# Two layers of a streaming encoder on one core: the MLP's down projection in passes of 512 hidden columns, with seven block products in place of eight

## What is computed

```python
D_MODEL, D_FF = 1024, 4096          # 1024 + 8 * 16 = 1152 tokens = 9 tiles of 128
def sq_relu_mlp(x, w_up, w_down):
    return jnp.square(jax.nn.relu(x @ w_up)) @ w_down
...
hp = hp + sq_relu_mlp(rmsnorm(hp, norm_ffn[i]), ffn_w_up[i], ffn_w_down[i])
hs = hs + sq_relu_mlp(rmsnorm(hs, norm_ffn[i]), ffn_w_up[i], ffn_w_down[i])
```

## Time and profile before

| | us |
|---|---|
| median of 3 runs | 2989.47 |
| lowest and highest run | 2988.71, 2990.20 |
| span of the profiled execution | 2987.3 |
| PE busy | 2903.7 (97%) |
| PEld busy | 2644.4 (89%) |
| DVE busy | 1504.3 (50%) |
| ACT busy | 996.1 (33%) |
| POOL busy | 683.6 (23%) |

### The profile page before, as it was taken

One profiled execution on the slowest core, in us unless ns is written; L12 is line 12 of the kernel. 1 busy time (PEld: TensorE's weight loads), 2 busy tenths in 40 slices (PEclk: granted clock), 3 DMA queues, 4 the chain that ended last, 5 costly groups with the idle time before them and its releaser, 6 DMA issues. The chain is left out here.

```text
span 2987.3 us, 44886 instructions
## 1 busy us (share of the span) xinstructions
PE 2903.7 (97%) x17447; PEld 2644.4 (89%) x17447; DVE 1504.3 (50%) x2576; ACT 996.1 (33%) x1796; POOL 683.6 (23%) x482
## 2 busy tenths in 40 slices
PE   8999999989999999999999999989999999999998
PEld 8889877679998999999989899978999999999997
DVE  4489799842544444434452266536253434343435
ACT  3377678761321212121231144433132121212122
POOL 2221110112212121111122244445221111111111
PEclk9999999999999999999999999999999999999999
DMA  4422612342211111111104333266211111111111
GB/s 146 110 69 72 170 36 43 64 151 75 66 42 42 42 42 42 42 42 42 42 14 149 104 98 107 89 237 217 73 64 42 42 42 42 42 42 42 42 42 64
DMA packets 196024, 222.38 MB, mean 74 GB/s; under 512 B 27745, under 2 KB 172065, under 8 KB 195890
## 3 DMA queue, kind: packets, MB, share of 16 engines
q1 hardware_dynamic: 155346, 156.08, 17.1%
q10 hardware_dynamic: 40544, 64.49, 6.6%
HBM read 170.58 MB, written 49.95 MB: 74 GB/s over the span
## 5 line engine op out<-in xcount | busy, mean ns | idle before, releaser
L918 DVE TENSOR_TENSOR h<-mlp_dn_acc,h 128x512 f32<-128x512 f32 x576 | 397.4, 691 | 339.6 <-PE mlp_dn_acc L873 339.6
L907 DVE TENSOR_TENSOR mlp_sq<-mlp_relu 128x384 f32<-128x384 f32 x192 | 163.6, 852 | 541.6 <-ACT mlp_relu L794 541.6
L858 PE MATMUL acc<-mid_xT_hi,mid_w_hi 128*128 128x384 f32 x752 | 251.4, 334 | 0.6 <-PEq L572 0.6
L858 PE MATMUL acc<-mid_xT_hi,mid_w_lo 128*128 128x384 f32 x752 | 251.4, 334 | 0.0
L858 PE MATMUL acc<-mid_xT_lo,mid_w_hi 128*128 128x384 f32 x752 | 251.3, 334 | 0.0
L873 PE MATMUL mlp_dn_acc<-mid_w_hi,mlp_hid_hi 128*128 128x512 f32 x576 | 224.6, 390 | 0.0
L873 PE MATMUL mlp_dn_acc<-mid_w_lo,mlp_hid_hi 128*128 128x512 f32 x576 | 224.5, 390 | 0.0
L873 PE MATMUL mlp_dn_acc<-mid_w_hi,mlp_hid_lo 128*128 128x512 f32 x576 | 224.4, 390 | 0.0
L873 PE MATMUL mlp_dn_acc<-end_w_lo,mlp_hid_hi 128*128 128x512 f32 x576 | 224.4, 390 | 0.0
L873 PE MATMUL mlp_dn_acc<-end_w_hi,mlp_hid_lo 128*128 128x512 f32 x576 | 224.3, 389 | 0.0
L873 PE MATMUL mlp_dn_acc<-end_w_hi,mlp_hid_hi 128*128 128x512 f32 x576 | 224.1, 389 | 0.0
(11 more groups left out here) (402 smaller groups left out, 7373.2 us busy)
## 6 DMA issues: line engine op xcount, KB each, us to landing
spare_w<-in_ffn_w_up ACTq DMA_DIRECT2D x30, 1024.0 KB, 5.3
mid_w_raw<-in_ffn_w_down ACTq DMA_DIRECT2D x15, 1024.0 KB, 5.0
end_w_raw<-in_ffn_w_down ACTq DMA_DIRECT2D x15, 1024.0 KB, 5.0
proj_w_raw<-in_a_w_in SPq DMA_DIRECT2D x8, 1024.0 KB, 6.0
mid_w_raw<-in_b_w_in SPq DMA_DIRECT2D x6, 1024.0 KB, 6.1
spare_w<-in_b_w_in SPq DMA_DIRECT2D x5, 1024.0 KB, 6.0
hd<-h SPq DMA_DIRECT2D x9, 512.0 KB, 9.5
state_g<-gg SPq DMA_DIRECT2D x9, 512.0 KB, 8.0
```

The source lines that it names most:

```text
L858: mm = pe.matmul(up_acc[:, u % 3, 0:GW], w_up_s[a][:, k, j * P:(j + 1) * P], x_s[c][:, k, g * GW:(g + 1) * GW], start=(n == 0), stop=(n == ...
L907: dve.tensor_tensor(sq[:, u % 2, :], relu[:, u % 2, :], relu[:, u % 2, :], ALU.mult)\
L918: dve.tensor_tensor(cols, dn_acc[:, v % 3, :], cols, ALU.add).then_inc(added, 1)
```

## The change

In 7 of 8 passes per phase, the down projection of the 1024 prompt tokens is made by a scheme with seven block products. A pass now takes 512 hidden columns (`FC` = 4 blocks of 128), and there are `NCH` = 8 passes; the loop covers six of them.

- The pass's down weights are cut in four blocks of 256 hidden by 512 output columns (B11, B12, B21, B22), the hidden block of 512 by 1024 tokens in four blocks A11 to A22 of 256 hidden by 512 tokens. Seven products of blocks or of sums of blocks (`H_OF`, `W_OF`) give what eight plain ones give. One product is four units (`t`) of 6 matmuls of 512 columns; products 1, 4 and 6 go on in the banks of the product before without clearing them. What is shared between outputs is collected in `U` over the passes and added to `h` in the last pass (12 adds of 128x512). The tile of sample tokens is made plainly: one unit more in products 0, 1, 5 and 6, in the `up_acc` banks.
- DVE makes four sums of weight blocks (`w_sum`) and four of hidden blocks (`h_sum`), 128x1024 each, both operands in SBUF; the low halves of the weights of products 0 and 1 (`weight_low`) and of all seven hidden operands (`hidden_low`), also 128x1024 with both operands in SBUF; four `sample_low` of 128x128; and 31 adds of 128x512.
- POOL makes the low halves of the weights of products 2 to 6 (128x1024 each) and of four blocks of up weights (128x8x128 each).
- ACT squares in place in float32 (`evacuate`), and makes the high halves of what is multiplied: two 128x1024 copies per product, four copies for the up weights, four of 128x128 for the sample tile.
- `up_acc` has two banks in place of three, `dn_acc` four.
- All loads of the phase are issued by SP, in the order `dn(0)` (two of 1 MB), `up(1)` (1 MB), the norm's gamma, and then pass by pass. ACT waits for both loads of `dn` before it evacuates unit 1.
- The last pass stays plain: 36 units of 6 matmuls, with the hidden operands and the weights in halves.
- Outside the phase only the places of buffers change (`early_1` and `gg_last` are freed earlier; `s_hi` of `mlp1` lies in `early_0`).

The core of the diff (indentation shortened):

```diff
-    NCH = FF // CW
-    FB = CW // P
-    UU = NG * FB
-    DU = NT * (D // 512)
+def mlp_phase(nc, name, sh, h, w_up, w_down, next_gamma, next_w=None, y=None, banks=None, pre=0, s_hi=None):
+    FC, W2, TB = 4, D // 2, NT_P // 2
+    NCH = FF // (FC * P)
+    UORD = ((0, 0), (1, 0), (0, 1), (0, 2), (1, 1), (1, 2), (2, 0), (2, 1), (2, 2), (3, 0), (3, 1), (3, 2))
+    UU = len(UORD)
+    AFTER = {f: max(u for u, (ff, _) in enumerate(UORD) if ff == f) + 1 for f in range(FC)}
+    NP = 7
+    ADDS = (5, 5, 4, 4, 4, 4, 5)
+    DU = sum(ADDS)
+    done_by = [sum(ADDS[:k]) for k in range(NP + 1)]
+    S_END = DU * (NCH - 1)
+    FIRST_HALF = [(0, t) for t in (0, 1, 2, 3, 4, 5, 6, 7, 8)] + [(1, t) for t in (8, 0, 1, 2, 3, 4, 5, 6, 7)]
+    N1 = len(FIRST_HALF)
...
+        up_acc = TwoSlots(*banks[:2])
+        dn_acc = TwoSlots(*(z if z is not None else b.ps(f"dn_acc{i}", [P, 512]) for i, z in enumerate(banks[2:])))
...
+        B11, B12, B21, B22 = raw_a[:, :, 0:W2], raw_a[:, :, W2:D], raw_b[:, :, 0:W2], raw_b[:, :, W2:D]
+        A11, A12, A21, A22 = hid[:, 0:2, 0:W2], hid[:, 2:4, 0:W2], hid[:, 0:2, W2:SEQ], hid[:, 2:4, W2:SEQ]
+        W_OF = (B11, B21, B11, B12, B21, t1[:, :, :], B22)
+        H_OF = (A11, A12, A11, s3, A22, A21, A12)
...
+    def up(s):
+        sp.dma_start(up_raw, up_src(s)).then_inc(up_in, 16)
+    def dn(i):
+        sp.dma_start(raw_a, dn_src(i, 0)).then_inc(dn_in, 16)
+        sp.dma_start(raw_b[:, :, :], dn_src(i, 1)).then_inc(dn_in, 16)
+    def body(i, first, last):
+        if not first:
+            sp.wait_ge(up_lo_done, FC * i)
+            up(2 * i + 1)
+        if not last or next_w is not None:
+            sp.wait_ge(up_lo_done, FC * i + 2)
+            if last:
+                sp.dma_start(up_raw, next_w.rearrange("(k p) n -> p k n", p=P)).then_inc(up_in, 16)
+            else:
+                up(2 * i + 2)
+        if not last:
+            sp.wait_ge(w_lo26_done, (NP - 2) * i + NP - 2)
+            dn(i + 1)
+    dn(0)
+    up(1)
     tail.load_gamma(sp)
+    passes(sp, body)
...
+    def evacuate(i, u, first):
+        f, g = UORD[u]
+        if not (first and u < pre):
+            act.wait_ge(up_done, UU * i + (u + 1 - pre))
+        if g < 2:
+            pieces_of = ((hid[:, f, g * GW:(g + 1) * GW], 0, GW),)
+        else:
+            if not (first and f < 2):
+                act.wait_ge(s_lo_done, FC * i + (f - 1))
+            pieces_of = ((hid[:, f, 2 * GW:SEQ], 0, 2 * P), (s_raw[:, f % 2, :], 2 * P, GW))
+        for dst, c0, c1 in pieces_of:
+            last = act.activation(dst, up_acc[:, u % 2, c0:c1], ACT.Relu)
+        last.then_inc(up_out, 1)
+        act.wait_ge(up_out, UU * i + (u + 1))
+        for dst, c0, c1 in pieces_of:
+            last = act.activation(dst, dst, ACT.Square)
+        last.then_inc(squared, 1)
...
+        evacuate(i, 0, first)
+        act.wait_ge(dn_in, 32 * i + 32)
+        if not first:
+            act.wait_ge(dn_done, DU * i)
+        weights(w_hi[:, 0, :, :], B21 if last else B11)
+        evacuate(i, 1, first)
+        weights(w_hi[:, 1, :, :], B22 if last else B21)
+        evacuate(i, 2, first)
+        evacuate(i, 3, first)
+        up_weights(i, 2)
+        sample(i, 0)
+        evacuate(i, 4, first)
+        act.wait_ge(squared, UU * i + 5)
+        hidden(0, A11)
+        evacuate(i, 5, first)
+        up_weights(i, 3)
+        sample(i, 1)
+        if last:
+            hidden(1, A21)
+        for u in (6, 7, 8):
+            evacuate(i, u, first)
+        if last:
+            weights(quarters(up_hi, 0), B11.rearrange("p f (q c) -> p f q c", c=P))
+        else:
+            up_weights(i, 4)
+        sample(i, 2)
+        evacuate(i, 9, first)
+        evacuate(i, 10, first)
+        if not last:
+            act.wait_ge(squared, UU * i + 11)
+            hidden(1, A12)
+        evacuate(i, 11, first)
+        if last:
+            weights(quarters(up_hi, 1), B12.rearrange("p f (q c) -> p f q c", c=P))
+        sample(i, 3)
+        if last:
             return
+        up_weights(i, 5)
+        for k in range(2, NP):
+            act.wait_ge(dn_done, DU * i + done_by[k - 1])
+            if k in (2, 6):
+                act.wait_ge(s_done, 4 * i + (3 if k == 2 else 4))
+            hidden(k % 2, H_OF[k])
+            if k in (2, 4):
+                act.wait_ge(w_sum_done, 4 * i + (3 if k == 2 else 4))
+            weights(w_hi[:, k % 2, :, :], W_OF[k])
...
+    def up_weights(i, f):
+        pool.wait_ge(up_hi_done, FC * i + (f - 1))
+        pool.tensor_tensor(up_half(up_lo, f % 2), up_half(up_raw, f % 2), up_half(up_hi, f % 2).bitcast(F32), ALU.subtract)\
+            .then_inc(up_lo_done, 1)
     def body(i, first, last):
+        up_weights(i, 2)
+        up_weights(i, 3)
         if not last or next_w is not None:
+            up_weights(i, 4)
+            up_weights(i, 5)
+        if not last:
+            for k in range(2, NP):
+                pool.wait_ge(w_hi_done, NP * i + k + 1)
+                pool.tensor_tensor(w_lo[:, k % 2, :, :], W_OF[k], w_hi[:, k % 2, :, :].bitcast(F32), ALU.subtract)\
+                    .then_inc(w_lo26_done, 1)
...
+            if not (first and u < 2):
+                pe.wait_ge(up_out, UU * i + (u - 1))
...
+    def product(dst, lhs, rhs, onto=False):
+        n = 0
+        for f in range(2):
+            for a, c in TERMS:
+                mm = pe.matmul(dst, lhs(c, f), rhs(a, f), start=(n == 0 and not onto), stop=(n == 2 * len(TERMS) - 1),
+                               skip_group_check=onto)
+                n += 1
+        return mm
...
+        for k in range(NP):
+            if k < 2:
+                pe.wait_ge(w_lo01_done, 2 * i + k + 1)
+            else:
+                pe.wait_ge(w_lo26_done, (NP - 2) * i + k - 1)
+            pe.wait_ge(h_lo_done, NP * i + k + 1)
+            if k == 5:
+                pe.wait_ge(up_out, UU * i + UU)
+                sample(k, 1, 0)
+            for t in range(TB):
+                if k >= 1:
+                    pe.wait_ge(added, DU * i + done_by[k - 1] + t + 1)
+                elif not first:
+                    pe.wait_ge(added, DU * i - ADDS[NP - 1] + t + 1)
+                product(dn_acc[:, t, :], lambda c, f: h_s[c][:, k % 2, f, t * P:(t + 1) * P],
+                        lambda a, f: w_s[a][:, k % 2, f, :], k in (1, 4, 6)).then_inc(dn_done, 1)
+            if k == 0:
+                pe.wait_ge(s_lo_done, FC * i + 2)
+                pe.wait_ge(up_out, UU * i + UU - 1)
+                sample(k, 0, 0).then_inc(dn_done, 1)
+            if k == 1:
+                pe.wait_ge(s_lo_done, FC * i + FC)
+                pe.wait_ge(added, DU * i + done_by[1])
+                sample(k, 0, 1, True).then_inc(dn_done, 1)
+            if k == 6:
+                sample(k, 1, 1, True).then_inc(dn_done, 1)
...
+    def adds(i, k, first):
+        n = DU * i + (done_by[k] + 1)
+        for t in range(TB):
+            dst = (U[:, t, :], cols(t, 0), U[:, t, :], cols(TB + t, 1), cols(TB + t, 0), cols(TB + t, 1), cols(t, 1))[k]
+            add(n + t, dst, dn_acc[:, t, :], first and k == 0)
+        if k in (0, 1, 6):
+            add(n + TB, cols(NT_P, (1, 0, 0, 0, 0, 0, 1)[k]), up_acc[:, k // 6, :])
...
+        dve.wait_ge(dn_in, 32 * i + 32)
+        w_sum(t1[:, :, :], B12, B11)
+        dve.wait_ge(w_sum_done, 4 * i + 1)
+        w_sum(B12, B22, B12)
+        weight_low(NP * i + 1, w_lo[:, 0, :, :], B11, w_hi[:, 0, :, :])
+        dve.wait_ge(w_lo01_done, 2 * i + 1)
+        w_sum(B11, B22, t1[:, :, :])
+        weight_low(NP * i + 2, w_lo[:, 1, :, :], B21, w_hi[:, 1, :, :])
+        dve.wait_ge(w_sum_done, 4 * i + 3)
+        dve.wait_ge(w_lo01_done, 2 * i + 2)
+        w_sum(B21, B21, B11)
+        sample_low(i, 0)
+        dve.wait_ge(squared, UU * i + 6)
+        h_sum(s3, A11, A21)
+        hidden_low(NP * i + 1, 0, A11)
+        sample_low(i, 1)
+        sample_low(i, 2)
+        dve.wait_ge(squared, UU * i + UU)
+        dve.wait_ge(s_done, 4 * i + 1)
+        h_sum(A21, A21, A22, ALU.add)
+        hidden_low(NP * i + 2, 1, A12)
+        dve.wait_ge(s_done, 4 * i + 2)
+        dve.wait_ge(h_lo_done, NP * i + 1)
+        h_sum(A11, A21, A11)
+        sample_low(i, 3)
+        dve.wait_ge(s_done, 4 * i + 3)
+        dve.wait_ge(h_lo_done, NP * i + 2)
+        h_sum(A12, A12, A11)
+        adds(i, 0, first)
+        for k in range(2, NP):
+            hidden_low(NP * i + k + 1, k % 2, H_OF[k])
+            adds(i, k - 1, first)
+        adds(i, NP - 1, first)```

How the instructions stand. First PE: one turn of the loop held 144 matmuls of 384 columns and 108 of 512, twice per 512 hidden columns; now it holds 288 and 192. DVE, in the loop of `mlp0`, from the end of the up part to the first operand of the down part's product 2 (`mlp_hid` is the hidden block, `mlp_both_u` is `U`, `mlp_h_lo` the low halves; L1110 is `h_sum`, L1104 `hidden_low`, L1096 `sample_low`, L1117 an add). Before:

```order
L906 REGISTER_ALU
```

(47 more changed lines are left out.)

246 lines of the change are left out of this document (130 added, 116 removed).

## The result

The changed kernel takes 2974.7 us (median of four runs, 2970.2 to 2978.4) against 2989.1 for the kernel before (2988.1 to 2990.2): 14.4 us less, ratio 0.9952 (95% interval 0.9936 to 0.9964). It is faster, as forecast, but by 14 us where the forecast had 32. The profiled execution is the slowest of the four, 2978.4 us with a span of 2976.6. It goes with the 2987.3 us of the earlier trace rows, so the two profiles are 10.7 us apart.

What follows compares the result with a forecast made beforehand. PE, busy 97% of the span, was taken to bound the kernel. Span 2987.3 - 76.3 (matmuls) + 33.6 (waits before product 1) + 10.5 (entries) = 2955.1 us, median 2957; 8-in-10 range 2919 to 2984.

Steps and rivals of the forecast that it cites:

- the side that had 0.86: Whole kernel: the measured time would be faster than before, chance 0.86, against 0.04 for same and 0.10 for slower.
- the forecast's own range: Whole kernel: 2945 to 2973 us, from a product 1 wait of 1.8 to 3.3 and entries of 8 to 15; chance 0.57.
- The matmuls: Down part: 24 matmuls fewer per pass at 0.227 us each, 5.45 us per pass, 76.3 us saved over 14 passes.
- The wait between products 0 and 1: Before product 1, PE waits 2.4 us per pass for DVE's first add, delayed by POOL's up block; 33.6 us in all.
- The alternation: Before product 1, queued POOL and DVE instructions take turns, so POOL's 2.40 us up block gets in between DVE's.
- The products after it: Products 2 to 6: operands are ready before PE comes, nothing lost, with 0.7 us in hand.
- case 3: Products 2 to 6: DVE falls behind POOL, 3.6 us more waiting per pass, 3007 us, slower than before; chance 0.10.
- The entries: Start of each phase: PE waits for ACT 0.96 us, then 4.3 us; 10.5 us over both phases, between 8 and 15.
- The clock: PE's granted clock in the passes and at the entries: the sum had no term for a drop behind waits.
- The case that did: Behind the 2.4 us wait in every pass, PE's clock drops, 1.6 us lost each: +22, 2979 us; chance 0.06.

## Why the prediction was wrong in its size

The result lies within the range (2919 to 2984) and on the side that had 0.86, but outside the forecast's own range (2945 to 2973).

**The matmuls.** Right in their number, 336 fewer, and a little too high in their worth: 72.4 us with the waits and drops taken away, for 76.3. A price of 0.227 us for every matmul left out that a group at the start of a product costs more (43.9 us of down matmuls per pass for the 43.6 forecast).

**The wait between products 0 and 1.** Right in its place, cause and number. 14 times 2.18 to 2.23 us, 30.7 us for 33.6. The 0.2 us less for each is of the order of what DVE saves on instructions in a row (1.14 us from one to the next, where one lasts 1.23). The alternation was read from the earlier trace rows, at other sizes and in another phase, and it held. The Trainium skill's rule (SBUF — State Buffer, "Who interferes with whom") agrees with the 3.42 us row, and with the 1.22 that is left when GpSimd is moved.

**The products after it.** Right: no wait. The reason that case 3 stays away is stronger than the one given. With the wait gone too, DVE met POOL in half of the passes and took its lead back each time.

**The entries.** Right in their length: 10.8 us for 10.5.

**The clock: this is the step that failed.** The sum charged nothing for it. The case that did was one of all or nothing, every pass or none, with a chance of 0.06. It came in part: 8 of 14 waits were followed by a drop (12.8 us), and both entries by a longer one, together 5.2 us. That is 18 us that the sum had at nothing, and most of what the forecast missed.

The two phases can be closed on the profiled executions. Each stretch below goes from PE's third up unit (the time it was ready for it) to the last down matmul; the first two are the kernel before, the others the changed one:

```profile
774.30:1568.70 794.40, 791.00 (x4033) 720.10 (x4032) 348.04 (x496) 172.28 (x252) 154.63 (x49) 1.00 0.13 43
2189.80:2979.10 789.30, 788.72 (x3985) 720.42 (x3984) 342.04 (x487) 164.40 (x239) 149.51 (x48) 1.00 0.14 46
```
```profile
778.40:1561.60 783.20, 761.06 (x3864) 693.38 (x3864) 411.03 (x440) 261.68 (x454) 176.08 (x84) 0.99 0.13 44
2183.30:2968.30 785.00, 764.59 (x3816) 696.79 (x3816) 405.48 (x430) 253.60 (x440) 171.13 (x82) 0.98 0.13 46
```

| | us |
|---|---|
| matmuls | -72.4 |
| waits before product 1 | +30.7 |
| waits at the entries | +10.8 |
| small waits (3.9 in the kernel before, 1.1 in the changed one) | -2.8 |
| clock behind the 14 waits | +12.8 |
| clock behind the entries | +5.2 |
| sum | -15.7 |
| the two phases in the profiles (1583.7 and 1568.2) | -15.5 |

The spans differ by only 10.7 us, because the phases that the change leaves alone took 4.7 us more in this execution, 4.1 of them before mlp0. Nothing was changed there. The stretch before mlp0 takes 774.3 to 777.7 us in the five profiles of the kernel before and its versions with waits, and 775.3 to 778.4 in the seven of the changed kernel and its versions. The pair compared here stands at the two ends, 774.3 and 778.4.

The median is 3.7 us lower than the profiled execution. The four runs of the changed kernel spread over 8 us, and one would expect some spread from a number of drops that differs between executions: the same 14 waits had 8 drops in one profile and 7 in another, and the drop behind the long wait of mlp1 cost 3.1 us in one and 1.7 in four others. But the kernel before, which has no drops in its phases, spread over 7 us in one group of seven runs too, so the spread alone shows nothing.

The evidence was on record. A drop behind an idle time of 4.17 us stands in the earlier trace rows, and the forecast put two idle times of 4.3 us into the kernel by its own working without charging them. What it set against the case was that no slice of the page lies lower and that at mlp0 the clock was 1.00. But the phases of the kernel before hold no wait of this length, so their clock says nothing of what one would do, and a slice of 75 us does not show a drop of 3.4 (the changed kernel's slices don't either). For 2.4 us, between "nothing" and the 1.6 us of the earlier trace rows, a middle value for each wait would have been a better term: 14 x 0.8 = 11 us, and 2 x 1.6 for the entries, gives 2971. This estimate is made after the fact. The Trainium skill (TensorE: Matmul & The Clock Gate, "Why this matters for your kernels") warns of idle gaps between bursts of matmuls. The runs agree that idle gaps cost clock, and show it for gaps shorter than that section names, 2.09 to 2.2 us. I had named the warning and given it no price in the sum.

## What to carry to other kernels

A wait put into a PE that was never idle has two prices, its length and the clock behind it. Both are read at the wait, in a stretch of 10 us behind it, not in the page's slices; and where the trace has no wait of that length, charge each new one a middle value rather than giving the clock a small all-or-nothing chance. In the kernel before, a wait of 1.2 us cost 1.5 us, one of 2.1 cost 3.1, and one of 3.0 cost 4.8. These prices were measured at one place, the sixth unit of the down part.

Where DVE is in a chain that PE waits for, look at what GpSimd is given in the same microseconds. One low half, needed by nobody for another 40 us, cost 41 us of this kernel's time (2974.7 to 2933.8), and it had only to be moved in GpSimd's own order.
